# Resident attention masks and a reordered first stage in a two-layer hybrid decoder step

## The chip, the cores and the metric

One core of a Trainium2 chip runs one launch of the program. The metric is device microseconds (us) of an execution, the median of three runs. TensorE (PE) does the matrix products, VectorE (DVE) and ScalarE (ACT) the elementwise work, GpSimd (POOL) small copies. SyncE (SP), ACT and POOL each issue transfers on a queue of their own, and the transfers of a queue are issued in the order of the program.

## The reference, cut to what matters

Two layers work on 288 tokens: a prompt of 256 and eight sequences of four new tokens. The weights are float32, and what matters of one layer is this:

```python
h = rmsnorm(x, norm_pre)
z, xbc, dt_raw, q, k, v, g_att, b_sc, c_sc, h_sc, g_sc = split(h @ w_in)
y_ssd = ssd_branch(z, xbc, dt_raw, ...)         # conv, chunked scan, gated group norm
y_att = swa_branch(q, k, v, g_att, k_buf, v_buf, ...)   # k rotated; window of 128 by additive masks
y_sc  = sc_branch(b_sc, c_sc, h_sc, g_sc, ...)
x = x + rmsnorm(concat(y_ssd, y_att, y_sc) @ w_out, norm_post)
x = x + sigmoid(x @ ple_gate) * (p @ ple_proj)
```

The rotated keys and the values are outputs too, and so are copies of the old key and value rows.

## The kernel before, in words

**Products.** A weight unit is 2048 x 128 of a weight matrix, 1 MB. There are 142 of them in a layer: four at first (two tiles of k, two of v), then 22 for each of four head groups g (numbered k = 0 to 21 in the code), 32 for the output projection, 2 and 16 for the embedding. A unit arrives in two halves of 512 KB in a ring of six `raw` buffers. ACT writes a rounded high part `whi` (`split_hi`), DVE the rest `wlo` (`split_lo`), and PE makes three products (high by high, high by low, low by high) for each of 16 row blocks (`product`, lines 473 to 475). So a unit is 48 products of 288 columns, and the sums go into one of two main PSUM banks in turn (`project`). Six more banks (A0, A1, YB, YO, T0, T1) serve all else.

**Order.** The order of the instructions on each engine is written out by hand, and semaphores tie the engines together. ACT and DVE split a unit's halves some two units ahead of PE: after unit k, `split_after` in ACT's loop handles the last half of unit k + 2 and the first of unit k + 3. A raw half is loaded on SP's queue as soon as PE has used the half six before it (`load_unit`, line 372). So anything else that SP waits for or issues stands in front of the next weights.

**First stage of a layer.** The two k units and the step-size weights run side by side, block by block, in main banks 0, 1 and T1; then the two v units follow in main banks 0 and 1, for which DVE must first have rotated the keys out of the same banks (`rotate`, lines 1220 to 1223). `step_sizes` (lines 1265 to 1292) is a chain of small DVE and ACT instructions. ACT stores the rotated keys to `kout` and the transposed values to `vout`, and copies the old rows (`kold`, `vold`) from DRAM to DRAM. Group 0 reads keys and values back from there.

**A group's beginning.** With unit k = 1 of each group (k = 2 of group 0) SP waits until the state of the group before is stored (line 404), and then loads the group's keys twice, the cached keys, and the masks, the same in every group, in ten transfers (lines 407 to 415). With k = 3 it loads values. At k = 0 of the next group ACT and DVE make the norm of the group before (`group_norm`: `rsqrt`, `normalise`), and only then does DVE rotate the first tile of queries out of main bank 0. PE runs `late_states` after k = 0 and k = 1 (line 541), and needs bank 0 for k = 2. After k = 2 it makes the attention scores of the rotated queries (line 556).

Of the kernel before, what the change touches and what calls it, by code (L numbers as in the profile page):

```python
# [23 lines left out]
P = 128  # L24
# [82 lines left out]
def hybrid_step(nc, wts, wdt, x0, p_t, npre, npost, gpar, dtpar, s0_t, kc_t, vc_t, cs_in, sc_in, consts, masks, resets,  # L107
                xs, kout, vout, kold, vold, conv_out, scv_out, ssm_p, ssm_s):
    ctx = ExitStack()
    with ctx:  # L110
# [43 lines left out]
        WK_N = 15360  # L154
# [34 lines left out]
        YT = cut(T)  # L189
        YS = cut(T)  # L190
# [8 lines left out]
        MSK = cut(3 * P + P + NSM)  # L199
        PT = WK[:, at[0] - (4 * P + NB * P + NSM):at[0] - NSM].rearrange("p (j n) -> p j n", j=4)  # L200
# [5 lines left out]
        OS = cut(2 * NSM).rearrange("p (a n) -> p a n", n=NSM)  # L206
        PR = cut(4 * 3 * P).rearrange("p (j n) -> p j n", j=4)
# [5 lines left out]
        DT0 = cut(T, HEAVY + 2400)  # L213
# [6 lines left out]
        RST = cut(T)  # L220
        HF = [cut(T) for _ in range(6)]
# [11 lines left out]
        assert 3 * KT * T + DTW <= WK_N and LATE >= 2 * KT * T + 7 * T and 2 * KT * T + UNIT - KT * T <= HEAVY + 2400  # L233
# [29 lines left out]
        YB, YO = Bank("yb", 1, 5, 3), Bank("yo", 1, 6, 2)  # L263
# [56 lines left out]
        def unit(L, k):  # L320
            return L * LAYER_U + k
# [4 lines left out]
        OUT_F = PRE_U // 2 + G * GRP_U // 2  # L326
# [38 lines left out]
        def _(sp):  # L365
# [19 lines left out]
            for L in range(0, DEPTH):  # L385
# [11 lines left out]
                for g in range(0, G):  # L397
                    for k in range(GRP_U):
                        load_unit(gunit(L, g, k))
                        if k == (1 if g else 2):  # L400
# [10 lines left out]
                            new = masks[0:NSM, NMASK - NSM:NMASK].unsqueeze(1).to_broadcast([NSM, 4, NSM])  # L411
                            sp.dma_start(MSK[:, 4 * P:4 * P + NSM], new).then_inc(msk_in, 16)
                            own = masks[0:NS, 3 * P:4 * P].unsqueeze(1).to_broadcast([NS, 4, P])
# [49 lines left out]
        def _(pe):  # L463
# [32 lines left out]
            for L in range(0, DEPTH):  # L496
# [21 lines left out]
                for k in (2, 3):  # L518
                    project(unit(L, k), k % 2, fill(L, k % 2, k // 2))

                def turn_values(i):
                    bk = (YB, YO)[i]
                    wait(v_ready, L * 2 + (i + 1))
                    wait(bk.free, bk.in_pre(L, 0))
# [22 lines left out]
                for g in range(0, G):  # L547
# [63 lines left out]
                    for k in range(GRP_U):  # L611
                        project(gunit(L, g, k), k % 2, fill(L, k % 2, (PRE_U + g * GRP_U + k) // 2))
# [183 lines left out]
        def _(act):  # L796
# [39 lines left out]
            for L in range(0, DEPTH):  # L836
# [11 lines left out]
                for k in range(PRE_U):  # L848
                    act.wait_ge(halves_used, used(unit(L, k)))
                    if k < 2:  # L850
                        swap(KSW[:, k, :], MAIN[k % 2]).then_inc(k_swapped, 1)
                    else:
                        fn(VTT[:, k - 2, :], MAIN[k % 2][:, 0:T], ACT.Copy).then_inc(v_ready, 1)
                        act.drain().then_inc(bank_free[k % 2], 1)
                    split_after(unit(L, k))
# [6 lines left out]
                    if k == 1:  # L862

# [7 lines left out]
                    if k == 2:  # L871
                        for i in range(2):
                            act.wait_ge(k_ready, L * 2 + (i + 1))
                            act.dma_start(kout[L, 2 * i:2 * i + 2].rearrange("h d n -> (h d) n"), KTT[:, i, :]).then_inc(k_stored, 16)
# [203 lines left out]
                def keep_mix(mp, m):  # L1078
# [3 lines left out]
                    if i == 7:  # L1082
                        act.wait_ge(state_stored, L * (G * 16) + (G * 16 + 16))
# [102 lines left out]
        def _(dve):  # L1186
# [61 lines left out]
            for L in range(0, DEPTH):  # L1248
# [45 lines left out]
                for k in range(PRE_U):  # L1294
# [4 lines left out]
                    if k == 0:  # L1299
                        step_sizes()  # L1300
# [546 lines left out]
```

## Time and profile before

| | |
|---|---|
| median of 3 runs | 2180.59 us (2180.2 to 2182.91) |
| the profiled execution | 2181.6 us, its span 2179.8 us |
| PE busy | 2062.8 us, 95% of the span |
| DVE busy | 1387.8 us, 64% |
| ACT busy | 1081.5 us, 50% |
| transfers | 367.25 MB, 168 GB/s over the span |
| mean granted TensorE clock | 0.979 of full |

A "wait" in the rows below is idle time of an engine that ended with an event of the one named as releaser. The granted clock has two levels, 1.2 and 2.4 GHz, shown as 0.5 and 1.0; a mean between them says how much of a stretch was at either.

### The profile page before, as it was taken

How to read it: one execution, taken by the hardware profiler on the slowest of the kernel's cores; microseconds unless marked ns; L12 is line 12 of the kernel's file. 1: busy time of each engine (PE TensorE's matmuls, PEld its weight loads, DVE VectorE, ACT ScalarE, POOL GpSimd, SP SyncE). 2: the span in 40 equal slices, each digit the busy share in tenths (PEclk: the TensorE clock that was granted, in tenths of full speed). 3: DMA queues.
4: the chain of work that ended last, by engine and by line, in shares of the span. 5: the costliest groups of instructions: out<-in, count | busy, mean ns of one | idle time of the engine just before them, and what ended most of it. 6: DMA issues, size and time to landing. Idle time of an engine off the chain costs nothing.

```text
span 2179.8 us, 39335 instructions
## 1 busy us (share of the span) xinstructions
PE 2062.8 (95%) x15582; PEld 1993.2 (91%) x15582; DVE 1387.8 (64%) x2339; ACT 1081.5 (50%) x2151; POOL 62.1 (3%) x141
## 2 busy tenths in 40 slices
PE   4899999999989999999968999999999999999999
PEld 4799899899989989999968998998998998999999
DVE  4567676677667774347554677676766777644575
ACT  4556455446455553345444564564554465433543
POOL 0000000001001000000000000000000010000000
PEclk9999999999999999999989999999999999999999
DMA  5654464455365455554536545644644553655544
GB/s 189 185 179 146 144 215 153 159 177 176 115 203 187 130 195 182 178 177 150 165 118 199 181 135 179 195 138 148 214 150 160 178 175 122 210 176 182 168 155 150
DMA packets 121279, 367.25 MB, mean 168 GB/s; under 512 B 31144, under 2 KB 37096, under 8 KB 119656
## 3 DMA queue, kind: packets, MB, share of 16 engines
q1 hardware_dynamic: 108464, 332.73, 47.4%
q10 hardware_dynamic: 12488, 29.65, 3.8%
q8 instruction: 123, 2.02, 0.4%
q0 software_dynamic: 144, 2.36, 0.3%
q14 instruction: 60, 0.49, 0.1%
HBM read 336.75 MB, written 32.01 MB: 169 GB/s over the span
## 4 chain that ended last, share of the span: by engine, by line
PE 85%; DVE 6%; ACT 2%; DMA 2%; SPq 1%; DVEq 1%; issue 1%; ACTq 1%
PE main L473 26%; PE main L475 25%; PE main L474 25%; DMA raw<-wts 2%; DVE wlo L1190 1%; PE yb L592 1%; DVE conv_sum L1428 1%; PE yo L607 1%; PE yo L596 1%; PE t L683 1%; ACTq L824 1%; DVEq L1602 1%; DVE y_or_x L1604 0%; SPq L415 0%; PE a L582 0%
## 5 line engine op out<-in xcount | busy, mean ns | idle before, releaser
L473 PE MATMUL main<-h_hi,whi 128*128 128x288 f32 x3952 | 1194.8, 302 | 65.1 <-DVE work L1220 28.6
L474 PE MATMUL main<-h_lo,whi 128*128 128x288 f32 x3952 | 1178.0, 298 | 0.0
L475 PE MATMUL main<-h_hi,wlo 128*128 128x288 f32 x3952 | 1174.1, 297 | 0.0
L1190 DVE TENSOR_TENSOR wlo<-raw,whi 128x1024 fp32r<-128x1024 f32 x568 | 692.0, 1222 | 450.1 <-ACT whi L806 436.1
L473 PEld LDWEIGHTS main<-h_hi,whi 128*128 128x128 f32 x3952 | 752.8, 190 | 85.6 <-DVE work L1220 32.0
L806 ACT ACTIVATE whi<-raw 128x1024 fp32r<-128x1024 f32 x568 | 576.7, 1053 | 378.9 <-DMA raw<-wts 210.9
L474 PEld LDWEIGHTS main<-h_lo,whi 128*128 128x128 f32 x3952 | 754.1, 191 | 3.2 <-issue 1.9
L475 PEld LDWEIGHTS main<-h_hi,wlo 128*128 128x128 f32 x3952 | 755.3, 191 | 0.0
L1428 DVE SCALAR_TENSOR_TENSOR conv_sum<-conv_in,gpar_sb,conv_sum 128x312 f32<-128x312 f32 x144 | 90.2, 626 | 113.8 <-ACT conv_sum L968 105.8
L475 PE MATMUL main<-yssd_hi,wlo 128*128 128x288 f32 x512 | 151.7, 296 | 0.0
L473 PE MATMUL main<-yssd_hi,whi 128*128 128x288 f32 x512 | 151.5, 296 | 0.0
L474 PE MATMUL main<-yssd_lo,whi 128*128 128x288 f32 x512 | 149.7, 292 | 0.0
L912 ACT ACTIVATE tanh<-main 128x288 f32<-128x288 f32 x64 | 26.3, 410 | 168.8 <-PE main L475 168.7
L474 PEld LDWEIGHTS main<-yssd_lo,whi 128*128 128x128 f32 x512 | 97.4, 190 | 0.1
L473 PEld LDWEIGHTS main<-yssd_hi,whi 128*128 128x128 f32 x512 | 96.2, 188 | 0.1
L475 PEld LDWEIGHTS main<-yssd_hi,wlo 128*128 128x128 f32 x512 | 96.1, 188 | 0.0
L964 ACT ACTIVATE conv_in<-conv_state_in 128x24 f32<-128x24 f32 x48 | 11.0, 228 | 162.5 <-PE main L475 162.5
L1341 DVE SCALAR_TENSOR_TENSOR work<-tanh,main 128x288 f32<-128x288 f32 x64 | 28.9, 452 | 93.4 <-ACT tanh L912 93.4
L1084 ACT ACTIVATE conv_sum<-main 128x288 f32<-128x288 f32 x32 | 13.1, 410 | 117.9 <-PE main L475 117.9
L1692 POOL COPY short_state_out<-conv_in 128x2 f32<-128x2 f32 x16 | 11.4, 711 | 1312.6 <-DVE conv_in L1408 1312.6
L815 ACT ACTIVATE work<-main 32x288 f32<-32x288 f32 x80 | 32.1, 401 | 30.4 <-PE main L475 29.3
L1313 DVE TENSOR_TENSOR work<-work,decay_last 128x512 f32<-128x512 f32 x64 | 43.8, 685 | 1.5
(272 smaller groups left out, 1754.6 us busy)
## 6 DMA issues: line engine op xcount, KB each, us to landing
raw<-wts SPq DMA_DIRECT2D x568, 512.0 KB, 3.7
work<-s_t SPq DMA_DIRECT2D x32, 512.0 KB, 5.3
ssm_s<-work ACTq DMA_DIRECT2D x8, 2048.0 KB, 8.8
y_or_x<-xs SPq DMA_DIRECT2D x16, 288.0 KB, 4.3
xs<-y_or_x ACTq DMA_DIRECT2D x2, 2016.0 KB, 7.6
y_or_x<-x SPq DMA_DIRECT2D x4, 576.0 KB, 6.1
xs<-y_or_x POOLq DMA_DIRECT2D x1, 2304.0 KB, 7.6
work<-kc_t SPq DMA_DIRECT2D x8, 256.0 KB, 4.0
```

The lines of the kernel that those rows point to most:

```text
L473: mm(out, w_hi, x_hi_, start=start, stop=False)
L474: mm(out, w_hi, x_lo_, start=False, stop=False)
L475: return mm(out, w_lo, x_hi_, start=False, stop=stop)
L592: last = mm(YB.t[64 * r:64 * r + 64, c * P:c * P + w], XDT[0:w, c, h * HD:(h + 1) * HD], m[0:w, c * P:c * P + w], start=True, stop=True)
L596: mm(YO.t[:, 0:P], S0[:, i * P:(i + 1) * P], XC[:, 1, P:2 * P], start=True, stop=True)
L806: fn(WHI[h % RING][:, :], RAW[h % RING][:, :], ACT.Copy).then_inc(hi_done, 1)
L815: last = fn(dst[a:a + 32, :], src[b:b + 32, 0:T], ACT.Copy)
L912: fn(TH[n % 2][:, 0:w], src, ACT.Tanh, scale=0.5).then_inc(th_ready, 1)
L1190: return tt(dst, raw, hi.bitcast(F32), ALU.subtract)
L1313: tt(stv, stv, DEC[:, :, 1 + b:2 + b].to_broadcast([P, HG, HD]), ALU.mult)
L1341: stt(dst, TH[n % 2][:, 0:T], 1.0, main[:, 0:T], ALU.add, ALU.mult).then_inc(th_used, 1)
L1428: last = stt(s[:, :], f[:, j:j + CW], GP[:, G_CW + 4 * t + j:G_CW + 4 * t + j + 1], s[:, :], ALU.mult, ALU.add)
```

## The change

The masks get a tile of their own and are loaded once, by POOL at the beginning. To make room in the work area, two scratch tiles (`YT`, `YS`) move into the norm vectors `RS` and `RA`. In the first stage the v units go to side banks YB and YO; ACT and DVE split the halves of the v units before they handle the keys. The stores of keys and values move from ACT's queue to SP's, each behind a wait for them; the copies of the old rows move to SP's queue at unit 8 of group 1. Group 0's keys are read from the tile on chip, with unit 1, and its values with unit 5.

```diff
-        WK_N = 15360
+        MSK = sb("masks_sb", 3 * P + P + NSM)
+        WK_N = 14816
...
-        YT = cut(T)
-        YS = cut(T)
+        YT, YS = RS[:, :], RA[:, :]
...
-        YB, YO = Bank("yb", 1, 5, 3), Bank("yo", 1, 6, 2)
+        YB, YO = Bank("yb", 2, 5, 3), Bank("yo", 2, 6, 2)
...
# SyncE, in the loop over g and k behind load_unit(gunit(L, g, k))
-                        if k == (1 if g else 2):
+                        if g == 0 and k == 1:
+                            sp.wait_ge(k_ready, L * 2 + 2)
+                            for i in range(2):
+                                sp.dma_start(kout[L, 2 * i:2 * i + 2].rearrange("h d n -> (h d) n"), KTT[:, i, :]).then_inc(k_stored, 16)
+                        if g == 0 and k == 3:
+                            sp.wait_ge(v_tok, L * 2 + 2)
+                            for i in range(2):
+                                for h in range(2):
+                                    v_h = VT[:, i, :].rearrange("p (c h d) -> p c h d", c=3, h=2)[:, :, h, :]
+                                    sp.dma_start(vout[L, 2 * i + h, 0:NPR].rearrange("(c p) d -> p c d", p=P), v_h[:, 0:2]).then_inc(v_stored, 16)
+                                    sp.dma_start(vout[L, 2 * i + h, NPR:T], v_h[0:NSM, 2]).then_inc(v_stored, 16)
+                        if g == 1 and k == 8:
+                            sp.dma_start(kold[L], kc_t[L].rearrange("g d (b w) -> (g d) b w", w=P)[:, :, NS:P]).then_inc(old_copied, 16)
+                            sp.dma_start(vold[L], vc_t[L][:, NS:P, :]).then_inc(old_copied, 16)
+                        if k == 1:
...
-                            sp.wait_ge(k_stored, L * 32 + 32)
-                            sp.wait_ge(tok_ready, L + 1)
+                            if g > 0:
+                                sp.wait_ge(k_stored, L * 32 + 32)
                             for r in range(2):
-                                sp.dma_start(KCUR[64 * r:64 * r + 64, :], kout[L, g]).then_inc(att_in, 16)
+                                sp.dma_start(KCUR[64 * r:64 * r + 64, :], kout[L, g] if g else KTT[0:64, 0, :]).then_inc(att_in, 16)
                             sp.dma_start(KC[0:64, :], kc_t[L, g]).then_inc(att_in, 16)
-                            sp.dma_start(MSK[:, 0:3 * P], masks[:, 0:3 * P]).then_inc(msk_in, 16)
...
-                            for b in range(NB):
-                                sp.dma_start(MSK[16 * b:16 * b + 16, 3 * P:4 * P], own).then_inc(msk_in, 16)
-                        if k == 3:
+                        if k == (3 if g else 5):
...
# TensorE
-                for k in (2, 3):
-                    project(unit(L, k), k % 2, fill(L, k % 2, k // 2))
+                for k, bk in ((2, YB), (3, YO)):
+                    wait(bk.free, bk.in_pre(L, 0))
...
# ScalarE, first stage
-                for k in range(PRE_U):
-                    act.wait_ge(halves_used, used(unit(L, k)))
-                    if k < 2:
-                        swap(KSW[:, k, :], MAIN[k % 2]).then_inc(k_swapped, 1)
...
+                first_half = 2 * unit(L, 0)
+                for h in (5, 6, 7):
+                    split_hi(first_half + h)
+                act.wait_ge(halves_used, used(unit(L, 1)))
+                for k in range(2):
+                    swap(KSW[:, k, :], MAIN[k]).then_inc(k_swapped, 1)
+                for k in range(4):
+                    split_hi(first_half + 8 + k)
...
-                            act.dma_start(kout[L, 2 * i:2 * i + 2].rearrange("h d n -> (h d) n"), KTT[:, i, :]).then_inc(k_stored, 16)
...
-                        act.dma_start(vout[L, 2 * i + h, 0:NPR].rearrange("(c p) d -> p c d", p=P), v_h[:, 0:2]).then_inc(v_stored, 16)
-                        act.dma_start(vout[L, 2 * i + h, NPR:T], v_h[0:NSM, 2]).then_inc(v_stored, 16)
...
-                act.dma_start(kold[L], kc_t[L].rearrange("g d (b w) -> (g d) b w", w=P)[:, :, NS:P]).then_inc(old_copied, 16)
-                act.dma_start(vold[L], vc_t[L][:, NS:P, :]).then_inc(old_copied, 16)
...
# VectorE, first stage
-                for k in range(PRE_U):
-                    split_after(unit(L, k))
-                    if k < 2:
...
+                for h in (4, 5, 6, 7):
+                    split_lo(first_half + h)
+                for k in range(2):
+                    dve.wait_ge(k_swapped, L * 2 + (k + 1))
+                    rotate(KTT[:, k, :], KSW[:, k, :], MAIN[k], k).then_inc(k_ready, 1)
+                step_sizes()
+                for k in range(4):
+                    split_lo(first_half + 8 + k)
...
-                                dve.wait_ge(msk_in, it(L, g, 10, 9) * 16)
+                                dve.wait_ge(msk_in, 160)
...
# GpSimd, once, behind its store of x
+            pool.dma_start(MSK[:, 0:3 * P], masks[:, 0:3 * P]).then_inc(msk_in, 16)
...
+            for b in range(NB):
+                pool.dma_start(MSK[16 * b:16 * b + 16, 3 * P:4 * P], own).then_inc(msk_in, 16)
```

## Rows read from the trace of the kernel before

**Rows 1.** The page, busy time, share of the span, instructions of PE
```profile
PE 2062.8 (95%) x15582; PEld 1993.2 (91%) x15582; DVE 1387.8 (64%) x2339; ACT 1081.5 (50%) x2151; POOL 62.1 (3%) x141
```

**Rows 2.** Waits of PE: waiter <- releaser: us in total, times, longest
```profile
PE main L473 <- DVE work L1220: 28.6, 10, 4.0
...
PE t L541 <- DVE rs_v L1211: 13.2, 6, 2.8
PE a L556 <- DVE work L1223: 11.3, 2, 5.8
...
PE main L473 <- DVE wlo L1190: 2.5, 3, 1.6
```

**Rows 3.** Timeline of PE: start, duration, instruction, idle before it and releaser
```profile
56.64 0.40 PE L473 MATMUL main<-h_hi,whi 128*128 128x288 f32 x1 [4.03 <-DVE work L1220]
...
99.74 0.81 PE L556 MATMUL a<-work 64*128 64x128 f32 x4 [5.46 <-DVE work L1223]
...
262.28 0.79 PE L541 MATMUL t<-x,b_masked 96*128 96x512 f32 x1 [1.94 <-DVE rs_v L1211]
...
266.05 0.61 PE L473 MATMUL main<-h_hi,whi 128*128 128x288 f32 x1 [2.98 <-DVE work L1220]
```

**Rows 4.** Windows of 10 us behind ten gaps: length, PE busy, granted clock, DMA
```profile
56.64:66.64 10.00, 8.51 (x50) 0.83 0.22 70
...
1690.88:1700.88 10.00, 10.00 (x58) 0.75 0.26 67
```

**Rows 5.** Timeline of SP's queue at the beginning of group 1
```profile
244.28 1.15 SPq L408 DMA_DIRECT2D work<-kout  x2
245.48 0.60 SPq L409 DMA_DIRECT2D work<-kc_t  x1
246.12 0.59 SPq L410 DMA_DIRECT2D work<-masks  x1
246.75 0.57 SPq L412 DMA_DIRECT2D work<-masks  x1
247.36 5.45 SPq L415 DMA_DIRECT2D work<-masks  x8
252.85 2.35 SPq L372 DMA_DIRECT2D raw<-wts  x4
```

**Rows 6.** Timelines of ACT and DVE in the same stretch
```profile
256.97 1.06 ACT L806 ACTIVATE whi<-raw 128x1024 fp32r<-128x1024 f32 x1 [9.48 <-PE main L475]
...
261.77 0.46 DVE L1211 TENSOR_TENSOR rs_v<-rs 128x288 f32<-128x288 f32 x1 [1.34 <-ACT rs L825]
...
265.61 0.39 DVE L1220 TENSOR_TENSOR work<-main,cst 128x288 f32<-128x288 f32 x1
...
271.81 0.45 DVE L1220 TENSOR_TENSOR work<-main,cst 128x288 f32<-128x288 f32 x1
```

**Rows 7.** Transfers: KB each, median us to landing; last row all weight halves
```profile
ssm_s<-work ACTq DMA_DIRECT2D x8, 2048.0 KB, 8.8
work<-kc_t SPq DMA_DIRECT2D x8, 256.0 KB, 4.0
...
DMA to landing us min/median/max: 3.4/3.7/9.6
```

**Rows 8.** Timelines of ACT and DVE in layer 0's first stage
```profile
52.24 1.64 ACT L815 ACTIVATE work<-main 32x288 f32<-32x288 f32 x4 [11.29 <-PE main L475]
...
57.40 0.50 DVE L1268 TENSOR_SCALAR work<-t,dt_params 32x288 f32<-32x288 f32 x1
...
63.52 2.34 DVE L1190 TENSOR_TENSOR wlo<-raw,whi 128x1024 fp32r<-128x1024 f32 x2
...
95.58 1.06 ACT L806 ACTIVATE whi<-raw 128x1024 fp32r<-128x1024 f32 x1 [6.08 <-DMA raw<-wts]
```

**Rows 9.** Layer 1: ACT's queue, then a window (columns as in rows 4)
```profile
1154.16 0.58 ACTq L894 DMA_DIRECT2D kold<-kc_t  x1
...
1168.00:1170.00 2.00, 2.00 (x17) 1.00 0.05 9
```

More of the change, by code:

```diff
@@ L212, in hybrid_step @@
         XSQ = cut(KT * T, 0)
-        DT0 = cut(T, HEAVY + 2400)
+        RST = cut(T, HEAVY)
+        HF = [cut(T) if i else cut(T, KT * T + DTW) for i in range(6)]
+        DT0 = cut(T, PR_AT)
         AC0 = cut(T)
@@ L517, in _ @@
                 last.then_inc(T1.full, 1)
-                for k in (2, 3):
-                    project(unit(L, k), k % 2, fill(L, k % 2, k // 2))
+                for k, bk in ((2, YB), (3, YO)):
+                    wait(bk.free, bk.in_pre(L, 0))
+                    for n in range(KT):
+                        wait_half(unit(L, k), n)
+                        last = product(bk.t[:, 0:T], unit(L, k), n, HHI, HLO, n, n == 0, n == KT - 1)
+                        if n % 8 == 7:
+                            last.then_inc(halves_used, 1)
+                    pe.sem_inc(bk.full, 1)
                 def turn_values(i):
@@ L523, in turn_values @@
                     wait(v_ready, L * 2 + (i + 1))
-                    wait(bk.free, bk.in_pre(L, 0))
+                    wait(bk.free, bk.in_pre(L, 1))
                     for c in range(3):
@@ L847, in _, with keep_values @@
                 fn(DTP[0:32, 2:3], DTP[0:32, 1:2], ACT.Exp)
-                for k in range(PRE_U):
-                    act.wait_ge(halves_used, used(unit(L, k)))
-                    if k < 2:
-                        swap(KSW[:, k, :], MAIN[k % 2]).then_inc(k_swapped, 1)
-                    else:
-                        fn(VTT[:, k - 2, :], MAIN[k % 2][:, 0:T], ACT.Copy).then_inc(v_ready, 1)
-                        act.drain().then_inc(bank_free[k % 2], 1)
-                    split_after(unit(L, k))
+                def keep_values(i):
+                    bk = (YB, YO)[i]
+                    act.wait_ge(halves_used, used(unit(L, 2 + i)))
+                    fn(VTT[:, i, :], bk.t[:, 0:T], ACT.Copy).then_inc(v_ready, 1)
+                    act.drain().then_inc(bk.free, 1)
+                first_half = 2 * unit(L, 0)
[6 more added lines that the diff above has]
+                    split_hi(first_half + 8 + k)
                     if k == 0:
@@ L1292, in step_sizes @@
                     tt(smp(DTE[0:32, NPR:T]), ac, ac[:, :, NS - 1:NS].to_broadcast([32, NB, NS]), ALU.subtract).then_inc(dt_ac, 1)
[L1294 to L1300 removed]
+                first_half = 2 * unit(L, 0)
+                for h in (4, 5, 6, 7):
[6 more added lines that the diff above has]
+                    split_lo(first_half + 8 + k)
                     if k == 1:
@@ L1668, in _ @@
             pool.dma_start(xs[0], YX[:, 0:KT * T]).then_inc(x_slab0, 16)
+            pool.dma_start(MSK[:, 0:3 * P], masks[:, 0:3 * P]).then_inc(msk_in, 16)
+            new = masks[0:NSM, NMASK - NSM:NMASK].unsqueeze(1).to_broadcast([NSM, 4, NSM])
+            pool.dma_start(MSK[:, 4 * P:4 * P + NSM], new).then_inc(msk_in, 16)
+            own = masks[0:NS, 3 * P:4 * P].unsqueeze(1).to_broadcast([NS, 4, P])
+            for b in range(NB):
+                pool.dma_start(MSK[16 * b:16 * b + 16, 3 * P:4 * P], own).then_inc(msk_in, 16)
             pool.wait_ge(const_in, 16)
```

34 lines of the change are left out of this document (13 added, 21 removed).

## The prediction, as it was put on record

> **What bounds the kernel now.** First the page: PE is busy for 2062.8 of 2179.8 us [rows 1], and 2062.8 us over 15582 products is 0.132 us each, so a unit of 48 takes 6.4 us. The other engines can only cost time through the 117 us in which PE is idle. So next the waits of PE [rows 2], and in PE's timeline where they lie [rows 3]. Four kinds are within reach of this change. The waits for L1220 (28.6 us in ten places) are for a rotation to free a main bank: three of them in the first stages, as at 56.64, the others at six beginnings of a group, as at 266.05. The waits of L541 (13.2 us, six places) are for the norm vector at the same six beginnings, as at 262.28. The waits of L556 (11.3 us, two places) are for the rotated queries at the end of each first stage, as at 99.74. Of the wait for `wlo`, 0.9 us stand in the first stages. Together 54.0 us: 32.3 at the beginnings of groups (13.2 and 19.1), 21.7 in the two first stages. The other waits of PE, some 60 us at the start, between layers and before the output projection, hang on code that the change leaves as it is.
>
> The granted clock adds to each gap. Behind the ten larger ones, windows of 10 us that begin where PE goes on show PE busy and the clock at 1.2 GHz for part of the time: a mean of 0.83 in the first, 0.75 in the last [rows 4], over all ten 0.785. Work at half clock takes twice as long, so a window loses 10 us times one minus its mean: 21.5 us over the ten, 13.7 of it behind the groups' beginnings and 7.8 in the first stages. If the gaps go, this goes too.
>
> **What holds a group's beginning.** At group 1 SP has passed its wait for the stored state at 244.28, issues the keys until 246.1, then ten mask transfers until 252.85, and only then the next half of weights [rows 5]. ACT's rounding of that half starts at 256.97, 4.1 us after the issue [rows 6]; the profile names PE as the releaser, but what this instruction needs of PE is the first half of unit 21, done long before, and at four of the other five beginnings the profile names the load at the same place. From there ACT and DVE run without a break, since the norm stands behind that rounding in ACT's order: 261.77 the vector that frees T1, 265.61 the rotation that frees main bank 0, 271.81 the second rotation, which the scores need [rows 6].
>
> **The masks, part by part.** Removed from SP at each beginning are ten issues, 246.12 to 252.85: 6.7 us [rows 5]. The half is then issued at 246.1, its ring place having been free since about 243, and the chain moves 6.7 us to the left. T1 is free at 255.5, where PE waited from 260.34: gone. Main bank 0 is free at about 259.3; PE, without its first wait, would want it at 266.05 - 2.98 - 1.94 = 261.1: gone, with 1.8 us to spare. The second rotation ends at about 273.2 - 6.7 = 266.5; PE is through unit 2 at 261.1 + 6.4 = 267.5: no wait, but only 1.0 us to spare. The six pairs of gaps are 4.9 to 5.7 us long, all less than 6.7.
>
> What the trace does not show is a half of weights issued right behind the keys (400 KB) on the same queue. Its landing is bounded by 3.4 us below and 9.6 above, the least and most of all halves [rows 7]; at 4.1 nothing is left, at 9.6 some 4.5 us of wait come back at each beginning, 27 in all. The cached keys themselves land in 4.0 us [rows 7], so I take about 4.5, and keep 2 us for the six together. Short waits of 0.9 and 1.5 us elsewhere were followed by no fall of the clock.
>
> A rule bears on this. The Trainium skill, "DMA: Bandwidth & Descriptors", section "Issuing engines are not separate DMA queues", says that all issuers share the same 16 DMA engines, and that issuing from another one saves only sequencer time, usually small beside the transfer. By it the masks' move would be worth almost nothing here, and the sum would be 46 us smaller. The row differs as to the size: 6.7 us of issuing stand before a half that lands in 4.1 us.
>
> POOL's ten mask transfers, once, cost nothing if they land before unit 3 of group 0, at about 91 us. They begin at about 21 us. Below stand SP's 6.7 us for the ten [rows 5], above ten times the slowest transfer in rows 7, 88 us, which would make one wait of up to 18 us. They are small like SP's, so I take the former. `YT` and `YS` in the norm vectors cost nothing: the same instructions on the same engine, and the next norm is computed only after the last use.
>
> **The first stage, part by part** (layer 0; layer 1 is alike). PE is through the k units at about 52.4 us. The halves of the v units are split before that, as ACT is idle for 11.29 us there [rows 8], and the banks are other ones, so the waits for L1220 (4.03 and 1.49 us here, 4.03 in layer 1) go. PE then works until 52.4 + 12.7 = 65.1. Meanwhile ACT copies both key tiles (1.64 us each [rows 8]) until 55.5; DVE rotates the second until 57.0, and runs `step_sizes` for 57.40 to 63.52, 6.1 us [rows 8], so until 63.1. Its split of the next half (1.2 us) is done at 64.3. That is 0.8 us before PE wants it: this edit has little cover, and each microsecond more in that chain is one of PE's, twice.
>
> The eight stores of values stood in front of ACT's splits and now stand in SP's queue, behind a wait for the transposes, which are ready about 4 us after unit 0 of the group ends (71.5), at 76. At the 0.58 us of a key load [rows 5] they take 4.6 us; the first half of unit 4 is then issued at 81 and lands at 85. PE wants it, split, at 92. ACT waits there for some 3 us, but has copied the second queries before, and the scores' unit 2 ends at 86. The ten masks are gone from this place too, and group 0's keys come from on chip. The half whose landing ended ACT's 6.08 us of idle at 95.58 [rows 8] is no longer needed before the queries, so the waits of L556 go: 11.3 us, and the 0.9 of `wlo`.
>
> **The copies of the old rows** (2 MB a layer) go from ACT's queue in the first stage to SP's, in front of weights. They are issued when PE ends unit 5 of group 1; the next half of weights is rounded by ACT after unit 6 and used by PE with unit 9, some 20 us later. Their length is bounded below by a store of as many bytes in 8.8 us [rows 7], above by 14 us: in layer 1 they are issued from 1154.16, and from 1168 the DMA engines stand at 0.05 [rows 9]. With the half behind them and its split that is 14 to 20 us, so hidden, at the upper end only just; ACT stalls, which delays the samples' softmax by less than PE's three units of lead. I take 0, and 2 us as the upper cost for both layers. The Trainium skill, same page, "Queues, rings and completion order", says that a DMA engine takes turns between queue rows but consumes one row's descriptors in order. By that rule the copies, which could interleave with weights before, now hold them up in full; no row here shows it, and it is the fourth case below.
>
> **The sum.** 54.0 + 21.5 - 2 = 73.5 us off the profiled execution's 2181.6 gives 2108.1. That execution is 1.0 us above the median, so 2107.
>
> **The rivals.**
> First, the beginnings of groups don't gain: the half behind the keys lands late, or the second rotation, with 1.0 us to spare, takes over. Then 21.7 + 7.8 = 29.5 us are gained, 2151; with half the gain 2129. For it speaks the little room; against it that the chain is 6.7 us shorter by SP's own rows.
> Second, the first stages don't gain: `step_sizes` or the stores in SP's queue hold up what the rotation did. Then only 46 - 2 = 44 us are gained, 2137; half of it, 2122. For it speaks the 0.8 us of cover; against it the 7 us that the values' stores have.
> Third, both together: 2180, no change.
> Fourth, slower: the copies hold up the weights of group 1. PE starts to wait when they take more than about 15 us, and loses from there one for one in each layer; it turns the sign only beyond 15 + 37 = 52 us. The 14 us of rows 9 speak against it.
>
> **How the numbers follow.** The forecast has 0.74, the first rival 0.12, the second 0.09, the third 0.02, the fourth 0.03. The forecast's own range is 2102 (no leftover, and the scores and late states at full clock too) to 2117 (a landing of some 6 us at the six beginnings). To leave out no more than two in ten the range reaches into the halves of the first two rivals: 2100 to 2135. A measurement of this kernel tells about 0.2% from no change, 4 us. Faster 0.95, no change 0.02, slower 0.03.
>
> **What would show it.** Right: no mask issues on SP's queue; ACT's rounding at a group's beginning some 4 us after SP's key loads; no wait of PE for L1220, L541 or the scores above 1 us, and a granted clock of 1.0 through all of a layer's groups. Wrong: PE waiting for `wlo` behind `step_sizes`; ACT idle for a half of weights behind the values' stores, or at units 6 to 8 of group 1, with PE waiting afterwards; or a new wait of the scores at unit 2. The prediction fails if PE's idle time behind these places stays above 20 us.

## The result, and the profile after

The changed kernel takes 2112.77 us (median of four runs, 2111.05 to 2114.97) against 2181.59 us of the kernel before in the same session: a ratio of 0.9685, 95% interval 0.9668 to 0.9702. It is 68.8 us faster; the point forecast was 2107, the range 2100 to 2135, so 5.8 us of the expected gain did not come.

The page of the changed kernel, span and busy times (the row that answers to [rows 1]):

```profile
span 2111.0 us, 39261 instructions
...
PE 2039.9 (97%) x15582; PEld 1974.7 (94%) x15582; DVE 1387.4 (66%) x2339; ACT 1082.6 (51%) x2151; POOL 66.0 (3%) x151
```

The span fell by 68.8 us, from 2179.8. PE's busy time fell by 22.9 with the same 15582 products, which is the clock (a mean of 0.994 where it was 0.979). The other 45.9 us are idle time of PE that is gone. The waits of PE in the changed kernel (columns as in [rows 2]):

```profile
PE main L482 <- DVE h_lo L1205: 15.2, 5, 6.0
PE t L509 <- DVE sq L1258: 13.5, 1, 13.5
PE main L482 <- DVE yssd_lo L1205: 13.0, 1, 13.0
...
PE main L482 <- DVEq L1434: 5.0, 2, 2.6
...
PE a L571 <- DVE work L1238: 2.0, 4, 0.5
...
PE main L482 <- DVE wlo L1205: 1.6, 1, 1.6
PE t L587 <- ACT work L1021: 1.3, 1, 1.3
```

The rotation was L1220 and is L1235 now; no wait of PE for it is left, nor one of the late states (L541, now L556) for the norm vector. The large rows are the ones at the start, between layers and before the output projection, which the change leaves as they are. Of the four kinds that the prediction summed, 2.0 us are left at the scores (L571) and nothing else. Two rows are new: 5.0 us for an event of DVE at L1434 and 1.3 us for ACT at L1021. The new waits in PE's timeline:

```profile
295.36 0.40 PE L482 MATMUL main<-h_hi,whi 128*128 128x288 f32 x1 [2.38 <-DVEq L1434]
...
419.75 0.50 PE L571 MATMUL a<-work 64*128 64x128 f32 x4 [0.52 <-DVE work L1238]
...
1341.79 0.40 PE L482 MATMUL main<-h_hi,whi 128*128 128x288 f32 x1 [2.64 <-DVEq L1434]
...
1349.94 0.43 PE L587 MATMUL t<-work 128*64 128x128 f32 x2 [1.27 <-ACT work L1021]
```

The three long ones, 6.3 us, lie in group 1 of each layer, in the units behind the copies of the old rows. The scores' wait at 419.75 has three more like it.

**A group's beginning.** SP's queue at the beginning of group 1 (answering to [rows 5]):

```profile
228.85 0.60 SPq L424 DMA_DIRECT2D work<-kc_t  x1
229.49 7.34 SPq L373 DMA_DIRECT2D raw<-wts  x4
```

ACT's rounding of the first half behind the keys, to set beside [rows 6]:

```profile
233.94 1.06 ACT L821 ACTIVATE whi<-raw 128x1024 fp32r<-128x1024 f32 x1 [3.25 <-DMA raw<-wts]
```

DVE's two rotations there:

```profile
242.59 0.39 DVE L1235 TENSOR_TENSOR work<-main,cst 128x288 f32<-128x288 f32 x1
...
248.79 0.45 DVE L1235 TENSOR_TENSOR work<-main,cst 128x288 f32<-128x288 f32 x1
...
249.69 0.46 DVE L1238 TENSOR_TENSOR work<-work 128x288 f32<-128x288 f32 x1
```

And PE's scores behind them:

```profile
250.20 0.50 PE L571 MATMUL a<-work 64*128 64x128 f32 x4
```

The weights now stand right behind the keys, and the half is rounded 4.45 us after its issue. From that rounding to the first rotation it is 8.65 us, as before (256.97 to 265.61 in [rows 6]): the chain was moved, not shortened. The second rotation is done at 250.15, and PE's scores begin at 250.20, so 0.05 us were to spare here. At the five later beginnings the same stretch from issue to rounding is 4.87, 5.23, 4.70, 4.43 and 5.09 us; the scores wait 0.5 us at the four that are longer than 4.45, and not at the one of 4.43.

**The first stage.** ACT's timeline in layer 0, answering to [rows 8]; the first row is the copies of the key tiles:

```profile
51.76 3.32 ACT L830 ACTIVATE work<-main 32x288 f32<-32x288 f32 x8 [3.22 <-PE main L484]
...
83.59 1.06 ACT L821 ACTIVATE whi<-raw 128x1024 fp32r<-128x1024 f32 x1 [1.75 <-DMA raw<-wts]
```

DVE's, with the first row of the step sizes and the splits behind them:

```profile
56.38 0.50 DVE L1283 TENSOR_SCALAR work<-t,dt_params 32x288 f32<-32x288 f32 x1
...
62.51 2.34 DVE L1205 TENSOR_TENSOR wlo<-raw,whi 128x1024 fp32r<-128x1024 f32 x2
```

And SP's queue with the first and the last of the eight stores of values:

```profile
74.79 0.40 SPq L410 DMA_DIRECT2D vout<-work  x1
...
78.99 0.47 SPq L411 DMA_DIRECT2D vout<-work  x1
79.50 0.90 SPq L373 DMA_DIRECT2D raw<-wts  x2
```

The step sizes run from 56.38, and the first of the two splits behind them ends at about 63.7, before PE is through the v units at some 64.7. The eight stores of values hold SP for 4.7 us, and the half behind them is rounded 4.1 us after its issue. PE waits for none of it.

### The profile page after: what moved, and what is told of

It is laid out like the page before. It is cut to its first block, busy times and chain, and to the rows that moved or that the text cites. A ratio compares the mean times of both kernels' runs of the same rounds, so it can differ in the third digit from the quotient of the medians.

```text
span 2111.0 us, 39261 instructions
## 1 busy us (share of the span) xinstructions
PE 2039.9 (97%) x15582; PEld 1974.7 (94%) x15582; DVE 1387.4 (66%) x2339; ACT 1082.6 (51%) x2151; POOL 66.0 (3%) x151
## 3 DMA queue, kind: packets, MB, share of 16 engines
q0 software_dynamic: 496, 2.64, 0.3%
## 4 chain that ended last, share of the span: by engine, by line
PE 83%; DVE 7%; DMA 4%; DVEq 2%; ACT 2%; SPq 1%; issue 1%; ACTq 1%
PE main L482 25%; PE main L484 24%; PE main L483 24%; DMA raw<-wts 3%; DVE wlo L1205 1%; DVE conv_sum L1445 1%; PE yb L607 1%; PE yo L622 1%; PE yo L611 1%; PE t L698 1%; DVEq L1619 1%; DVE y_or_x L1621 1%; ACTq L839 0%; PE a L597 0%; DVEq L1331 0%
## 5 line engine op out<-in xcount | busy, mean ns | idle before, releaser
L482 PE MATMUL main<-h_hi,whi 128*128 128x288 f32 x3888 | 1166.3, 300 | 40.5 <-DVE h_lo L1205 15.2
L483 PE MATMUL main<-h_lo,whi 128*128 128x288 f32 x3888 | 1150.9, 296 | 0.0
L484 PE MATMUL main<-h_hi,wlo 128*128 128x288 f32 x3888 | 1147.5, 295 | 0.0
L482 PEld LDWEIGHTS main<-h_hi,whi 128*128 128x128 f32 x3888 | 732.7, 188 | 58.1 <-issue 27.8
L483 PEld LDWEIGHTS main<-h_lo,whi 128*128 128x128 f32 x3888 | 733.9, 189 | 3.3 <-issue 1.9
L484 PEld LDWEIGHTS main<-h_hi,wlo 128*128 128x128 f32 x3888 | 735.5, 189 | 0.0
L927 ACT ACTIVATE tanh<-main 128x288 f32<-128x288 f32 x64 | 26.3, 411 | 150.0 <-PE main L484 150.0
L1165 ACT ACTIVATE tanh<-main 128x288 f32<-128x288 f32 x30 | 12.3, 409 | 60.6 <-PE main L484 55.7
```

The lines of the kernel that those rows point to most:

```text
L482: mm(out, w_hi, x_hi_, start=start, stop=False)
L483: mm(out, w_hi, x_lo_, start=False, stop=False)
L484: return mm(out, w_lo, x_hi_, start=False, stop=stop)
L927: fn(TH[n % 2][:, 0:w], src, ACT.Tanh, scale=0.5).then_inc(th_ready, 1)
```

## The experiments

All medians stand against the changed kernel's 2112.8 us where nothing else is said; ratios are to the kernel before.

**The two parts alone.** The first run is the kernel before with the resident masks and `YT`, `YS` in the norm vectors, and nothing of the first stage:

```
-        YT = cut(T)
-        YS = cut(T)
+        YT, YS = RS[:, :], RA[:, :]
...
-                            for b in range(NB):
-                                sp.dma_start(MSK[16 * b:16 * b + 16, 3 * P:4 * P], own).then_inc(msk_in, 16)
...
+            for b in range(NB):
+                pool.dma_start(MSK[16 * b:16 * b + 16, 3 * P:4 * P], own).then_inc(msk_in, 16)
```

> The kernel before with only the masks made resident (the changed tile layout, loaded once by GpSimd); first stage, stores and copies as before. Theory, that ten mask issues on SyncE hold the next half of weights wherever they stand: the six beginnings of groups gain 32.3 us of idle and 13.7 us of clock less some 2 us of short waits for the scores, and the end of each first stage, where the same ten issues stand before unit 3 of group 0, gains most of its 11.3 us with some 3 us of clock as well: about 2124 us. Rival, that masks count at the beginnings of groups alone and the scores of the first stage wait for the stores on ScalarE: 2181.6 - 44 = 2138 us.

The second is the changed kernel with the ten mask loads per group back on SP:

```
                             sp.dma_start(KC[0:64, :], kc_t[L, g]).then_inc(att_in, 16)
+                            sp.dma_start(MSK[:, 0:3 * P], masks[:, 0:3 * P]).then_inc(msk_in, 16)
...
+                            for b in range(NB):
+                                sp.dma_start(MSK[16 * b:16 * b + 16, 3 * P:4 * P], own).then_inc(msk_in, 16)
```

> The changed kernel with the masks loaded by SyncE in every group again, behind the cached keys. Theory: the waits of TensorE for the norm vector and for the first rotation come back at six beginnings of groups, 4.9 to 5.7 us each, with 1.5 to 2.9 us of clock: 44 us more than the changed kernel, about 2157 us, and the first stages stay without waits, as there the masks now stand two units earlier. Rival, that the gain at the beginnings came from elsewhere (the stores and copies off ScalarE's queue, the moved tiles): within 10 us of the changed kernel.

Masks alone gave 2131.55 us (0.9765, 0.9749 to 0.9782), the first stage alone 2160.83 (0.9903, 0.9889 to 0.9918): 50.0 and 20.8 us gained, 70.8 together, where the whole change gained 68.8. So the parts add up, and the masks are the larger. The stage-only time is close to the expected one, 48 us above the changed kernel where 44 were forecast. The masks-only time misses the theory (2124) by 7.5 us and lies about halfway to the rival (2138): in this kernel the waits at the beginnings are gone but for 0.5 us at the scores in three places, as the theory says, but the first stage kept most of its own. PE's timeline there:

```profile
55.42 0.61 PE L468 MATMUL main<-h_hi,whi 128*128 128x288 f32 x1 [4.04 <-DVE work L1215]
...
97.16 0.81 PE L551 MATMUL a<-work 64*128 64x128 f32 x4 [3.67 <-DVE work L1218]
```

The scores' wait at the end of the first stage was 5.46 before [rows 3]. The ten masks that left this place took 1.8 us of it; a half of weights issued at 82.26, rounded only at 92.99, kept the rest. ACT's rounding of it:

```profile
92.99 1.06 ACT L801 ACTIVATE whi<-raw 128x1024 fp32r<-128x1024 f32 x1 [4.27 <-DMA raw<-wts]
```

In the stage-only kernel the first stage has no waits, and the waits of the beginnings are all back:

```profile
246.05 0.49 PE L562 MATMUL t<-x,b_masked 96*128 96x512 f32 x1 [2.43 <-DVE rs_v L1232]
...
249.82 0.61 PE L488 MATMUL main<-h_hi,whi 128*128 128x288 f32 x1 [3.28 <-DVE work L1241]
```

Its six pairs sum to 33.8 us (32.3 before), with a granted clock of 0.66 in the 10 us from 246.

**What of the masks costs: bytes or issues?** Two runs put a part of the loads back in front of the weights, for groups 1 to 3: the one mask of 192 KB, or the eight of 8 KB.

```
+                            if g > 0:
+                                sp.wait_ge(msk_in, 160)
+                                sp.wait_ge(msk_more, (L * (G - 1) + g) * 16)
+                                sp.dma_start(MSK[:, 0:3 * P], masks[:, 0:3 * P]).then_inc(msk_more, 16)
```

> The changed kernel with one mask transfer, the largest (192 KB of the 272 KB that the ten had), issued again by SyncE behind the cached keys in groups 1 to 3. Theory, that the issue time on SyncE is what counted at the beginnings of groups: 0.6 us each, and as the chain has no room left there (four waits of 0.5 us for the scores in the changed kernel), about 0.6 times six: 3 to 5 us more than the changed kernel, 2116 to 2118 us. Rival, that it was the bytes or descriptors of the masks in the DMA engines: most of the loss comes back, over 2135 us.

```
+                                own = masks[0:NS, 3 * P:4 * P].unsqueeze(1).to_broadcast([NS, 4, P])
+                                for b in range(NB):
+                                    sp.dma_start(MSK[16 * b:16 * b + 16, 3 * P:4 * P], own).then_inc(msk_more, 16)
```

> The changed kernel with the eight small mask transfers (8 KB each, 64 KB in all) issued again by SyncE behind the cached keys in groups 1 to 3. Theory, issue time: eight issues of 0.63 us put the next half of weights 5.0 us later; the two waits of TensorE come back at some 4 us in each of six places with 1.5 to 2.5 us of clock: 33 to 40 us more, 2146 to 2153 us. Rival, bytes: a quarter of the loss at most, under 2125 us.

The eight small ones: 2148.29 us (0.9848, 0.9835 to 0.9862), 35.5 more, as the issue time says. SP's queue shows it:

```profile
229.49 5.50 SPq L431 DMA_DIRECT2D masks_sb<-masks  x8
235.04 3.01 SPq L374 DMA_DIRECT2D raw<-wts  x4
```

The half behind them is rounded 4.05 us after its issue here, and 4.0 to 4.2 us after it at all six beginnings, which is no longer than in the changed kernel:

```profile
239.09 1.06 ACT L828 ACTIVATE whi<-raw 128x1024 fp32r<-128x1024 f32 x1 [8.53 <-DMA raw<-wts]
```

So for the small masks it is the issuing that costs.

The one large load: 2122.99 us (0.973, 0.9717 to 0.9744), 10.2 more and so above the 2116 to 2118 that its issue alone would give. (Its profiled execution, the fastest of four, took 2119.6 us, 6.7 more than that of the changed kernel.) In the profile the six issues put the weights 4.6 us later in all. The time from the weights' issue to the rounding is 4.55, 5.84, 4.77, 4.68, 5.25 and 6.74 us at the six beginnings, where the changed kernel has 4.45, 4.87, 5.23, 4.70, 4.43 and 5.09: 3.1 us more in all, from three of the six. SP's queue at the worst of them, the beginning of group 3 in layer 1:

```profile
1614.11 0.53 SPq L429 DMA_DIRECT2D masks_sb<-masks  x1
1614.68 6.85 SPq L374 DMA_DIRECT2D raw<-wts  x4
```

And the rounding there in ACT's timeline:

```profile
1621.42 1.06 ACT L826 ACTIVATE whi<-raw 128x1024 fp32r<-128x1024 f32 x1 [6.02 <-DMA raw<-wts]
```

That what the large load carries makes the weights later is possible, but not shown: in the run without the copies of the old rows (below), which has no mask load on SP, the same stretch is 6.37 us at one beginning. By the medians the theory is 5 us short for the large load and the rival 12 too high; where the rest of the 10.2 us comes from stays open.

**Where the missing 6 us are: the copies of the old rows.** First the changed kernel without them:

```
-                        if g == 1 and k == 8:
-                            sp.dma_start(kold[L], kc_t[L].rearrange("g d (b w) -> (g d) b w", w=P)[:, :, NS:P]).then_inc(old_copied, 16)
-                            sp.dma_start(vold[L], vc_t[L][:, NS:P, :]).then_inc(old_copied, 16)
```

> The changed kernel without the two copies of old key and value rows; those two outputs are left unwritten. It prices the copies in all. Theory: the waits of TensorE at units 8 to 10 of group 1 go, 6.3 us: about 2106.5 us. Rival, that those waits have another cause (the softmax of the samples at that place in ScalarE's order): unchanged at 2111 to 2114 us.

2105.08 us (0.9648, 0.9634 to 0.9662): the copies cost 7.7 us, and the waits behind them are gone. In the changed kernel one sees how. SP's queue in group 1 of layer 0:

```profile
272.86 0.59 SPq L413 DMA_DIRECT2D kold<-kc_t  x1
273.49 3.14 SPq L414 DMA_DIRECT2D vold<-vc_t  x1
276.68 8.94 SPq L373 DMA_DIRECT2D raw<-wts  x4
```

ACT's rounding of the first of these four halves:

```profile
292.53 1.06 ACT L821 ACTIVATE whi<-raw 128x1024 fp32r<-128x1024 f32 x1 [12.27 <-DMA raw<-wts]
```

And DVE behind it:

```profile
293.62 1.23 DVE L1205 TENSOR_TENSOR wlo<-raw,whi 128x1024 fp32r<-128x1024 f32 x1 [8.50 <-ACT whi L821]
294.76 0.41 DVE L1432 SCALAR_TENSOR_TENSOR work<-conv_sum,main 128x256 f32<-128x256 f32 x1
```

The half behind the copies, the first of unit 9, is rounded 15.8 us after its issue, and its split by DVE ends at 294.85. What DVE does next, L1432, empties main bank 1, and PE goes on at 295.36. The unit that PE begins there is unit 9 itself: counted off in PE's trace it is the 36th unit of the layer, four at first, 22 of group 0 and the tenth of group 1. PE was through with unit 8 at 292.97. So it waited for these very weights until 294.85, some 1.9 of the 2.38 us, and then 0.5 us more for the bank, whose emptying stands behind their split. In layer 1 it is the same: PE wanted unit 9 at 1339.15, and its split ended at 1341.27.

Is it the order of SP's queue? The next run issues the same two copies at the same moment on ACT's queue (there the place is k = 5 of group 1):

```
+                        if g == 1 and k == 5:
+                            act.dma_start(kold[L], kc_t[L].rearrange("g d (b w) -> (g d) b w", w=P)[:, :, NS:P]).then_inc(old_copied, 16)
+                            act.dma_start(vold[L], vc_t[L][:, NS:P, :]).then_inc(old_copied, 16)
```

> The changed kernel with the two copies of old rows issued at the same moment of group 1 on ScalarE's queue instead of SyncE's. In the changed kernel TensorE waits 2.4 us in layer 0 and 2.6 and 1.3 us in layer 1 at units 8 to 10 of group 1, where ScalarE stood 12.3 us for a half of weights issued behind the copies. Theory, that the weights stand behind the copies in one queue: on the other queue they take turns, the waits go, about 2107 us. Rival, that the 2 MB take the same DMA engines whatever the queue: waits of the same size stay, 2111 to 2114 us.

2112.89 us (0.9684, 0.9669 to 0.9698), nothing gained, and in layer 0 the weights, on a queue without the copies, are rounded 18.2 us after their issue:

```profile
294.45 1.06 ACT L818 ACTIVATE whi<-raw 128x1024 fp32r<-128x1024 f32 x1 [11.03 <-DMA raw<-wts]
```

The theory fell: the order within SP's queue is not what makes them late. But the equal time is no proof that the order costs nothing. In layer 1 the half came 13.0 us after its issue, and PE did not wait for unit 9; other waits took the place, as one of 1.50 us in layer 0 at L575, while ACT has the issuing of the copies to do, 4.4 us there. Is it the form of the copy? Its slowest dimension is four groups. The next run splits it into four copies of 16 equal rows, at the same place on SP's queue:

```
-                            sp.dma_start(vold[L], vc_t[L][:, NS:P, :]).then_inc(old_copied, 16)
+                            for h in range(G):
+                                old, kept = (t.rearrange("w c -> (w c)").rearrange("(e f) -> e f", e=16) for t in (vc_t[L, h][NS:P, :], vold[L, h]))
+                                sp.dma_start(kept, old).then_inc(old_copied, 16)
```

> The changed kernel with the copy of old values cut into four transfers of 16 equal rows each (one for each head group) instead of one transfer whose slowest dimension is 4; same bytes, same place and queue. On ScalarE's queue at the same moment the copies cost as much as on SyncE's, so it is the DMA engines that they hold up. Theory, that the one transfer runs on few of the 16 engines, so that a half of weights, which needs all of them, waits for the slowest: spread out, the copies are over in about half the time, ScalarE's 12 us without a half of weights shrink below 6, and the waits at units 8 to 10 of group 1 go: about 2106 us. Rival, that it is the 2 MB (or the copy of keys in pieces of 496 bytes): waits of the same size, 2111 to 2114 us.

2104.8 us (0.9646, 0.9632 to 0.9659): the same bytes cost nothing that can be told from leaving them out. The half behind them, issued at 278.88, is rounded after 8.3 us instead of 15.8; ACT still stands 7.1 us for it, where I expected less than 6, but PE does not wait:

```profile
287.16 1.06 ACT L823 ACTIVATE whi<-raw 128x1024 fp32r<-128x1024 f32 x1 [7.13 <-DMA raw<-wts]
```

Windows of 4 us of the changed kernel behind the copies (length, busy times of PE, PEld, DVE, ACT and POOL, granted clock, DMA share, GB/s):

```profile
284.00:288.00 4.00, 4.00 (x34) 4.00 (x33) 1.03 (x3) 0.00 (x0) 0.00 (x0) 1.00 0.83 292
288.00:292.00 4.00, 4.00 (x32) 4.00 (x31) 0.00 (x0) 0.00 (x0) 0.00 (x0) 1.00 0.67 237
```

The same windows with the wide form:

```profile
284.00:288.00 4.00, 4.00 (x34) 4.00 (x33) 0.80 (x2) 0.84 (x1) 0.00 (x0) 1.00 1.00 405
288.00:292.00 4.00, 4.00 (x32) 4.00 (x31) 3.41 (x6) 2.84 (x6) 0.00 (x0) 1.00 0.94 354
```

While the narrow copy is under way and ACT waits for weights, the engines are not all at work: a share of 0.83 and 0.67, where the wide form has 1.00 and 0.94. The Trainium skill, "DMA: Bandwidth & Descriptors", section "Why a DMA increments its semaphore by 16 and not by 1", says that a transfer uses the largest number of engines up to 16 that divides the slowest dimension of both sides; by that the copy of four groups would run on four and each of the new ones on 16. The time and the shares agree with it; no row here shows the single engines. The nearest is a window of the masks-only kernel (same columns), where the narrow copy was issued at 73.38 and the half of 82.26 lands only at 92.91:

```profile
90.00:92.90 2.90, 2.87 (x21) 2.87 (x22) 0.00 (x0) 0.00 (x0) 0.00 (x0) 1.00 0.26 99
```

A share of 0.26 is that of some four of the 16 engines, and a half of weights has still to land there. The run with the wide form changes two things at once, the slowest dimension and the number of transfers (four for one), and no run separates them.

**The copies at their old place.** The changed kernel with the narrow copies back on ACT's queue at the end of the first stage:

```
+                act.dma_start(kold[L], kc_t[L].rearrange("g d (b w) -> (g d) b w", w=P)[:, :, NS:P]).then_inc(old_copied, 16)
+                act.dma_start(vold[L], vc_t[L][:, NS:P, :]).then_inc(old_copied, 16)
+
                 def group_norm(g):
```

> The changed kernel with the two copies of the old rows back at their former place, on ScalarE's queue at the end of the first stage, everything else kept. Theory (wherever the copies run, a half of weights that is loaded beside them lands some 10 us late, and the queries at the end of the first stage have no more slack than units 8 to 10 of group 1): PE waits 2 to 4 us near the scores of group 0 in each layer, 2110 to 2118. Rival (with the stores of values on SyncE and the keys taken on chip the late half is hidden there): no wait, 2104 to 2106, as without the copies.

2106.27 us (0.9649, 0.9636 to 0.9663). My theory fell but for small waits for `wlo`, of 0.73 us in layer 0 and 1.42 in layer 1; no scores wait there. So with the other edits in, the first stage hides the narrow copy but for these two waits, and moving it to group 1 lost 6.5 us. And in the kernel with masks alone, where the first stage was not reordered, the wide form was put at the old place, as its only edit:

```
-                act.dma_start(vold[L], vc_t[L][:, NS:P, :]).then_inc(old_copied, 16)
+                for h in range(G):
+                    old, kept = (t.rearrange("w c -> (w c)").rearrange("(e f) -> e f", e=16) for t in (vc_t[L, h][NS:P, :], vold[L, h]))
+                    act.dma_start(kept, old).then_inc(old_copied, 16)
```

> The kernel before with resident masks (2131.6) and, as its only other edit, the copy of the old value rows as four transfers of 16 equal rows at the same place. Theory (the narrow copy makes the halves beside it late, and this is most of what is left of the scores' wait of 3.67 and 3.25 us at the end of the first stage): these waits shrink to below 1 us, 2120 to 2126. Rival (that wait comes from ScalarE's order of work, with the stores of values in front of its splits): they stay above 2 us, 2130 to 2133.

2121.11 us (0.9721, 0.9708 to 0.9734), 10.4 less than masks alone, as the theory says, and the scores' waits of 3.67 and 3.25 us are gone but for 0.43 in layer 1; in layer 0 a wait of 1.92 us for `wlo` took the place of one of 0.95, and one of 1.68 for the second rotation that of one of 0.32. The same half of weights is rounded 5.3 us after its issue in layer 0, where it was 10.7. So with the masks out of the way, what the scores waited for was mostly this copy. In the kernel before it was not yet: there SP issues the half only behind the ten masks, when the copy is over or nearly so (the DMA share is 0.19 from 88 to 90),

```profile
91.18 0.91 SPq L372 DMA_DIRECT2D raw<-wts  x2
```

and it is rounded at 95.58 [rows 8], 4.4 us later. The masks stood in front of the copy's cost and hid it.

**The parts of the first stage.** The changed kernel with the v units in the main banks again:

```
-        YB, YO = Bank("yb", 2, 5, 3), Bank("yo", 2, 6, 2)
+        YB, YO = Bank("yb", 1, 5, 3), Bank("yo", 1, 6, 2)
...
-                for k, bk in ((2, YB), (3, YO)):
...
+                for k in (2, 3):
+                    project(unit(L, k), k % 2, fill(L, k % 2, k // 2))
```

> The changed kernel with the three V units of the first stage back in the main banks, fills as before the change, everything else kept. Theory (the order of the halves ahead of the rotation is most of the gain of the first stage, the side banks little): PE waits about 2 us per layer for a main bank, 2115 to 2119. Rival (the side banks are what removed the first stage's waits): the 4.0 us wait at unit 2 is back in both layers with the clock's loss behind it, about 2125 to 2130.

And with the stores of keys and values on ACT's queue again:

```
+                    act.wait_ge(v_tok, L * 2 + (i + 1))
+                    for h in range(2):
+                        v_h = VT[:, i, :].rearrange("p (c h d) -> p c h d", c=3, h=2)[:, :, h, :]
+                        act.dma_start(vout[L, 2 * i + h, 0:NPR].rearrange("(c p) d -> p c d", p=P), v_h[:, 0:2]).then_inc(v_stored, 16)
+                        act.dma_start(vout[L, 2 * i + h, NPR:T], v_h[0:NSM, 2]).then_inc(v_stored, 16)
```

> The changed kernel with the stores of group 0's keys and values issued by ScalarE again, everything else kept. Theory (ScalarE has the time at this point, so that the move of the stores hides): its roundings at unit 0 of group 0 come 0 to 2 us late per layer, 2112 to 2117. Rival (the move of the stores to SyncE is what freed the end of the first stage): 6 to 8 us per layer, about 2125 to 2129.

The first took 2119.3 us (0.9717, 0.9703 to 0.973), 6.5 more, just above the expected 2115 to 2119. PE waits for the rotation in four places, two in the first stages and two at beginnings of a group in layer 0:

```profile
53.89 0.40 PE L482 MATMUL main<-h_hi,whi 128*128 128x288 f32 x1 [1.82 <-DVE work L1228]
...
246.76 0.40 PE L482 MATMUL main<-h_hi,whi 128*128 128x288 f32 x1 [0.93 <-DVE work L1228]
```

The 4.03 us of before [rows 3] are 1.82 with the new order of ACT's and DVE's work and the old banks; the side banks take the rest. Why two beginnings came to wait too is not settled; at both the half behind the keys was rounded 6.2 us after its issue, against 4.45 and 5.23 in the changed kernel. The second took 2114.27 us (0.9699, 0.9686 to 0.9712), no difference that can be told from the changed kernel. In layer 0 ACT issues the stores of values from 73.61 to 79.28 and rounds the next halves at 79.60 where it was 74.93, and PE waits 0.24 us for a split.

**A version that beats both.** The wide copy, and the keys loaded behind unit 2's halves instead of in front of them (k = 2 in groups 1 to 3):

```
-                        if k == 1:
+                        if k == (2 if g else 1):
```

> As the run with the copy of old values in 16 rows, and in groups 1 to 3 SyncE waits for the stored state and loads the keys behind the halves of unit 2 instead of in front of them. Theory, that the next half's issue still starts the chain at a group's beginning: it is issued some 3 us earlier, when its ring place is free, the four waits of 0.5 us for the scores go, and the keys still land 10 us before the scores: 2 us less than that run, about 2104 us. Rival, that the keys are then late for the scores, or the chain is held by something else: no change or slower.

2100.57 us (0.9631, 0.9618 to 0.9644), 12.2 less than the changed kernel, 4.2 less than the wide copy alone (2 were expected) and the fastest of all. SP's queue at group 1:

```profile
222.14 7.19 SPq L373 DMA_DIRECT2D raw<-wts  x3
229.44 1.15 SPq L425 DMA_DIRECT2D work<-kout  x2
```

ACT's rounding of the half that used to stand behind the keys:

```profile
229.97 1.05 ACT L823 ACTIVATE whi<-raw 128x1024 fp32r<-128x1024 f32 x1
```

ACT finds the half there and doesn't wait. DVE's second rotation is done at 246.15, 3.3 us before PE's scores at 249.49, where it had 0.05 to spare. The idle time of PE is 62.8 us against 71.1, which is 8.3 less: the 6.3 at the copies and the 2.0 at the scores. The other 3.9 us are PE's busy time, 2036.0 us against 2039.9.

## Why the prediction was right, and where it was off

The bill: 54.0 us of waits within reach, less 6.3 and 2.0 of new and left ones, plus 22.9 of clock makes 68.6; the span fell by 68.8.

- **Groups' beginnings: shown.** The forecast was 46 us less a leftover of 2. Masks alone gave 50.0, of which some 4.3 came at the scores of the two first stages (5.46 to 3.67 and 5.80 to 3.25). The landing behind the keys, taken as 4.5, was 4.4 to 5.2 from issue to rounding. The leftover of 2 us was 2.0, at the place named: the second rotation, whose 1.0 us to spare was 0.05 at one beginning and nothing at four. The first rival is out.
- **The rule on issuing.** The sum by the rule would have been 46 us smaller. Eight issues of 5.50 us in all, each of 8 KB, cost 35.5 us over six places; here the issue time is what stands on the path. The one load of 192 KB cost 10.2 us where its six issues make 4.6, so issue time is not shown to be all of it.
- **First stages: the waits went as forecast.** Nothing is left of the 21.7 us. The cover of 0.8 us behind the step sizes held, the values' stores had slack as said, and the run with the stores back on ACT shows that moving them was not needed in the changed kernel. What I had incomplete is the reason for the scores' wait there: I put it to the stores in front of ACT's splits and to the masks. The masks held the half in the kernel before, but behind them stood a second cause that the prediction does not name, the narrow copy beside the weights, which kept 6.9 of the 11.3 us when the masks were gone. The run with the wide form in the masks-only kernel shows it, and that the stores, still on ACT there, kept next to nothing. The splits ahead of the rotation were not run without the rest, and neither were group 0's keys from on chip: how much of the gain is theirs stays open.
- **The clock: 21.5 forecast, 22.9 measured**, though not quite as described: the mean over the 10 us from 295.36, behind the new gap, is 0.83, which takes some 1.7 us back.
- **The copies: the mis-sized term.** I took 0 for them, 2 us at the most; they cost 6.3 us of waits in the profile and 7.7 by the run without them. The step that failed is the bound on their length: 14 us was read from how soon the DMA engines were idle in layer 1 [rows 9], where no half of weights was issued behind the copies until they were over, and that is not how long a half beside them needs. From the first copy's issue at 272.86 to the end of the half's split at 294.85 it was 22.0 us, and 22.2 in layer 1, where I had 14 to 20. The cover was right: PE wanted unit 9 at 292.97, 20.1 us after that issue, where I had some 20. What I did not count is the 0.5 us in which the bank is emptied behind the split, and the 1.27 us of waiting for ACT in layer 1. So my own sign of being wrong, ACT idle for a half of weights at units 6 to 8 of group 1 with PE waiting afterwards, did appear. The fourth rival's place was right and its size small. Its reason, the order within SP's queue, was not the main one: on ACT's queue the copies cost the same, and in 16 rows on SP's queue nothing.

## What to carry to other kernels

Here small transfers on a full queue cost at least their issue time at each place where a load that the chain waits for stands behind them; look at what is issued ahead of that load, and put behind it what is not urgent. When a transfer moves, bound the delay of what follows it from a place where something did follow it; how soon the DMA engines are idle again is no such bound. A wait that goes can uncover another cause behind it, as the masks did with the copy. For copies from DRAM to DRAM it is worth trying another form: as four transfers of 16 rows in place of one with a slowest dimension of four, the same bytes disappeared from the time here.

## What the runs showed of the hardware that was not expected

- A copy of 992 KB with a slowest dimension of four held a half of weights for 15.8 us from issue to rounding, and left ACT idle for 12.27 us on one queue and 11.03 on the other; in the form of 16 rows it was 8.3 us, with ACT idle for 7.13, and PE did not wait.
- The granted clock fell behind one of two like gaps. In the changed kernel it was 0.83 in the 10 us from 294, which begin within the gap of 2.38 us in layer 0, and 1.00 through the two stretches with the gaps of 2.64 and 1.27 us in layer 1:

```profile
294.00:304.00 10.00, 8.64 (x54) 8.43 (x55) 9.32 (x20) 7.92 (x16) 0.33 (x2) 0.83 0.53 195
...
1340.00:1350.00 10.00, 6.94 (x51) 6.65 (x52) 9.27 (x20) 8.00 (x17) 0.33 (x2) 1.00 0.58 205
1350.00:1360.00 10.00, 10.00 (x93) 9.45 (x94) 5.46 (x10) 5.41 (x14) 0.75 (x3) 1.00 0.55 166
```
